# FFN up as seven block products a pair, down summed in PSUM with reloaded features

## What is computed

```python
    h2 = _rmsnorm(x, g_pre_ffn) * (1 + sc2) + sh2
    up = _dwconv_rows(jnp.einsum('bld,df->blf', h2, w_up), conv_w, conv_b, grid)
    ug, uv = jnp.split(up, 2, axis=-1)
    f = jnp.einsum('blf,fd->bld', jax.nn.gelu(ug) * uv, w_down)
    x = x + gt2 * _rmsnorm(f, g_post_ffn)
```

## Time and profile before

| | us |
|---|---|
| three runs, median (lowest to highest) | 1947.3 (1946.1 to 1949.46) |
| the profiled execution | 1945.96 |
| its span, first to last instruction | 1944.2 |
| TensorE busy in it | 1890.8 |
| VectorE, ScalarE, GpSimd busy | 1028.4, 625.3, 86.5 |
| mean granted TensorE clock | 0.994 |

### The profile page before, as it was taken

One profiled execution on the slowest core, in us unless ns is written; L12 is line 12 of the kernel. 1 busy time (PEld: TensorE's weight loads), 2 busy tenths in 40 slices (PEclk: granted clock), 3 DMA queues, 4 the chain that ended last, 5 costly groups with the idle time before them and its releaser, 6 DMA issues.

```text
span 1944.2 us, 25592 instructions
## 1 busy us (share of the span) xinstructions
PE 1890.8 (97%) x10466; PEld 1764.1 (91%) x10466; DVE 1028.4 (53%) x2249; ACT 625.3 (32%) x1125; POOL 86.5 (4%) x125
## 2 busy tenths in 40 slices
PE   7999999999999999999999899999999999999995
PEld 2899999999999999999988899989989989989984
DVE  2662455455555543463545655555555555555557
ACT  3623222323233243451334442322323223223222
POOL 1000000000000100010000100000000000000003
PEclk9999999999999999999999899999999999999998
DMA  9122323223323343383222111111111111111104
GB/s 338 44 83 92 71 78 102 67 91 114 101 73 111 113 105 114 121 281 111 87 98 87 63 46 33 55 34 43 44 44 35 53 44 33 44 35 53 44 33 173
DMA packets 165401, 164.87 MB, mean 85 GB/s; under 512 B 5816, under 2 KB 141524, under 8 KB 165284
## 3 DMA queue, kind: packets, MB, share of 16 engines
q1 hardware_dynamic: 150356, 108.28, 19.0%
q0 software_dynamic: 10432, 37.17, 5.7%
q10 hardware_dynamic: 4496, 17.77, 2.3%
HBM read 131.48 MB, written 31.72 MB: 84 GB/s over the span
## 4 chain that ended last, share of the span: by engine, by line
PE 90%; DVE 6%; ACT 2%; DMA 1%; issue 1%; SPq 0%; ACTq 0%; DVEq 0%
PE ps L707 21%; PE ps L709 21%; PE ps L708 21%; PE ps L962 5%; PE ps L1033 4%; PE ps L1035 4%; PE ps L1034 4%; PE ps L843 2%; PE ps L846 2%; PE ps L845 1%; PE ps L749 1%; DVE H_lo L1468 1%; PE ps L822 1%; DVE acc L1862 1%; PE ps L734 1%; DMA adaw<-in_w_ada_dram 1%
## 5 line engine op out<-in xcount | busy, mean ns | idle before, releaser
L707 PE MATMUL ps<-H_hi,ring_hi 128*128 128x384 f32 x2328 | 797.3, 342 | 6.6 <-DVE H_lo L1468 4.5
L709 PE MATMUL ps<-H_hi,ring_lo 128*128 128x384 f32 x2328 | 779.8, 335 | 0.0
L708 PE MATMUL ps<-H_lo,ring_hi 128*128 128x384 f32 x2328 | 779.7, 335 | 0.0
L707 PEld LDWEIGHTS ps<-H_hi,ring_hi 128*128 128x128 f32 x2328 | 438.3, 188 | 12.0 <-DVE H_lo L1468 6.8
L708 PEld LDWEIGHTS ps<-H_lo,ring_hi 128*128 128x128 f32 x2328 | 438.6, 188 | 1.5
L709 PEld LDWEIGHTS ps<-H_hi,ring_lo 128*128 128x128 f32 x2328 | 438.1, 188 | 0.0
L1840 DVE TENSOR_TENSOR acc<-ps,acc 128x512 f32<-128x512 f32 x198 | 135.1, 689 | 101.5 <-PE ps L1035 101.5
L1468 DVE TENSOR_TENSOR ring_lo<-raw,ring_hi 128x1024 fp32r<-128x1024 f32 (+1 forms) x129 | 152.1, 1188 | 55.9 <-ACT ring_hi L1118 47.3
L1033 PE MATMUL ps<-ring_hi,fT_hi 128*128 128x512 f32 x396 | 156.8, 396 | 10.6 <-DVE acc L1840 8.2
L1034 PE MATMUL ps<-ring_lo,fT_hi 128*128 128x512 f32 x396 | 154.5, 390 | 0.0
L1035 PE MATMUL ps<-ring_hi,fT_lo 128*128 128x512 f32 x396 | 154.5, 390 | 0.0
(11 more groups left out here) (236 smaller groups left out, 1942.4 us busy)
## 6 DMA issues: line engine op xcount, KB each, us to landing
...
```

Of the source, the lines that this page charges most:

```text
L707: pe.matmul(out, whi, xhi, start=first, stop=False)
L708: pe.matmul(out, whi, xlo, start=False, stop=False)
L709: return pe.matmul(out, wlo, xhi, start=False, stop=last)
```

## The change

The weights and activations of one up feature form a product of a 2 x 2 block matrix with a 2 x 2 block matrix: gate and value columns by the two halves of the channels (A11, A12 for gate, A21, A22 for value), and the two halves of the channels by the two halves of the tokens (576 each, `HT`). The last 19 features (`NP`) are made with seven block products in place of eight (Strassen's scheme in Winograd's form). A product has 4 k x 3 matmuls, each over two runs of 288 columns (`SB`) that lie in two neighbouring banks; four such bank pairs are used in turn (`SLOT_BANK`). Features 0 to 2 stay plain products of 384 columns (`PLAIN`).

New work: eight sums of 128x576 for each of four k give the token-side quarters T1 to T4 (`quarter_tiles`, k=3 on VectorE, k=0 to 2 on GpSimd), with hi and lo parts. Four sums of 128x512 a feature give the weight side (`weight_sum`, GpSimd). The seven weights of a pair are split into `up_hi` and `up_lo`, during the pair before. ScalarE copies product 0 out (`hold`), VectorE adds the others to SBUF tiles `held` in seven sums of 576 (`output_sum`). The middle tap (ScalarE, `mid`) and the outer taps (VectorE, two SBUF tiles in) then work on halves of 576 tokens. Gate after gelu and value are stored to DRAM apart (`z_gate`, `z_value`), in four transfers a feature.

Down comes after all of up. For each third of the tokens (r) all 22 features are read back, 384 tokens of gate and of value, and w_down's 128 rows too (so three times in all): VectorE multiplies gate and value and makes the lo parts, ScalarE the hi parts, in rings of four. Three token tiles are summed in three bank pairs over all 22 features without going to SBUF. The last four features of the last third are done tile by tile (`down_end`). The final norm reads PSUM. acc, its memset and the 198 adds are gone. The residual is loaded by GpSimd.

```diff
+PLAIN = 3
+NP = NF - PLAIN
+HT = T // 2
+SB = HT // 2
...
+    SLOT_BANK = (0, 6, 2, 4)
...
+    def product_freed(eng, g):
+
+        s, i = g // 7, g % 7
+        if i == 0:
+            eng.wait_ge(product_held, s + 1)
+        else:
+            eng.wait_ge(output_summed, 7 * s + (i if i < 4 else i + 1))
...
+    def quarter_tiles(eng, done, k, before):
...
+        first, second = slice(0, HT), slice(HT, T)
+        as_f32 = lambda ap: ap.bitcast(F32)
+        x1, x2 = [[as_f32(h[:, k, c]) for h in (H_hi, H_lo)] for c in (first, second)]
+        y1, y2 = [[as_f32(h[:, KD // 2 + k, c]) for h in (H_hi, H_lo)] for c in (first, second)]
+        t1, t2, t3, t4 = [T_full[name][:, k, :] for name in quarters]
+        steps = ((t1, x2[0], x2[1], ALU.add), (t2, y2[0], y2[1], ALU.add), (t3, t2, t1, ALU.subtract),
+                 (t1, t1, x1[0], ALU.subtract), (t1, t1, x1[1], ALU.subtract), (t2, t2, t1, ALU.subtract),
+                 (t4, y1[0], t2, ALU.subtract), (t4, t4, y1[1], ALU.add))
+        for n, (out, a, b, op) in enumerate(steps):
+            if n:
+                eng.wait_ge(done, before + n)
+            eng.tensor_tensor(out, a, b, op).then_inc(done, 1)
...
+            for s in range(NP):
+                if s + 2 < NP:
+                    sp.wait_ge(up_lo_done, 7 * (s + 1))
+                    up_load(s + 2)
+                elif s == NP - 2:
+                    down_load(0)
+                    down_load(1)
+                    f_load(0)
+                else:
+                    down_load(2)
...
-            pool.wait_ge(done2, NT)
-            pool.memset(acc[:, :, :], 0.0).then_inc(acc_zero, 1)
...
+            def weight_sum(s, n):
+
+                a11, a12 = up_raw[s % 2][:, 0, 0:512], up_raw[s % 2][:, 0, 512:1024]
+                a21, a22 = up_raw[s % 2][:, 1, 0:512], up_raw[s % 2][:, 1, 512:1024]
+                if n == 0:
+                    pool.wait_ge(gate_in[s % 2], 16 * (s // 2 + 1))
+                    pool.wait_ge(value_in[s % 2], 16 * (s // 2 + 1))
+                    if s:
+                        pool.wait_ge(up_lo_done, 7 * (s - 1) + 6)
+                    else:
+                        pool.wait_ge(lo_ready, S_FF + 2 * PLAIN)
+                else:
+                    pool.wait_ge(weight_sums, 4 * s + n)
+                if n >= 1:
+                    pool.wait_ge(up_lo_done, 7 * s + ((2, 1, 4) if s else (0, 1, 2))[n - 1])
+                out, a, b, op = ((up_s1[:, :], a21, a22, ALU.add), (a21, a11, a21, ALU.subtract),
+                                 (a11, up_s1[:, :], a11, ALU.subtract), (a12, a12, a11, ALU.subtract))[n]
+                pool.tensor_tensor(out, a, b, op).then_inc(weight_sums, 1)
...
+            pool.wait_ge(h_split_done, 2 * NB * KD)
+            for n, k in enumerate(range(KD // 2 - 1)):
+                quarter_tiles(pool, pool_sums, k, 8 * n)
+                if n == 0:
+                    for j in range(4):
+                        weight_sum(0, j)
+            for s in range(1, NP):
+                for j in range(4):
+                    weight_sum(s, j)
...
+            def product(s, i, xhi, xlo, k0, c0):
...
+                else:
+                    product_freed(pe, g - 4)
+
+                pe.wait_ge(up_lo_done, g + 1)
+                for k in range(KD // 2):
...
+                    for n, (wt, x) in enumerate(((up_hi[i], xhi), (up_hi[i], xlo), (up_lo[i], xhi))):
+                        for sb in range(2):
+                            cols = slice(c0 + sb * SB, c0 + (sb + 1) * SB)
+                            mm = pe.matmul(ps[:, bank + sb, 0:SB], wt[:, w], x[:, k0 + k, cols],
+                                           start=(k == 0 and n == 0), stop=(k == KD // 2 - 1 and n == 2))
+                mm.then_inc(product_done, 1)
+
+            def up_pair(s):
+                product(s, 0, H_hi, H_lo, 0, 0)
+                product(s, 1, H_hi, H_lo, KD // 2, 0)
+                if s == 0:
+                    pe.wait_ge(quarter_lo, KD // 2)
+                product(s, 2, T_hi["T2"], T_lo["T2"], 0, 0)
+                product(s, 3, T_hi["T3"], T_lo["T3"], 0, 0)
+                product(s, 4, T_hi["T1"], T_lo["T1"], 0, 0)
+                product(s, 5, T_hi["T4"], T_lo["T4"], 0, 0)
+                product(s, 6, H_hi, H_lo, KD // 2, HT)
...
+            def down_tile(n, j):
+
+                k, r = down_cell(n)
+                q = TB * r + j
+                bank = SLOT_BANK[(7 * NP + q) % 4]
+                if k == 0:
+                    if q >= 4:
+                        pe.wait_ge(evac2, NT + q - 3)
+                    else:
+                        product_freed(pe, 7 * NP - 4 + q)
+                tok = slice(j * P, (j + 1) * P)
+                for x, w, first, last in ((f_hi, down_hi, True, False), (f_hi, down_lo, False, False), (f_lo, down_hi, False, True)):
...
+                        mm = pe.matmul(ps[:, bank + hb, :], x[n % DR][:, tok], w[n % DR][:, hb * 512:(hb + 1) * 512],
+                                       start=(k == 0 and first), stop=(k == NF - 1 and last))
+                return mm
+
+            def down_feature(n):
+
+                k, r = down_cell(n)
+                pe.wait_ge(down_ready, n + 1)
+                for j in range(TB):
+                    mm = down_tile(n, j)
+                    if k == NF - 1:
                         mm.then_inc(done2, 1)
+                if k < NF - 1:
+                    mm.then_inc(down_used, 1)
+
+            def down_end():
+
+                for j in range(TB):
+                    for n in range(NB * NF - DR, NB * NF):
+                        if j == 0:
+                            pe.wait_ge(down_ready, n + 1)
+                        mm = down_tile(n, j)
+                    mm.then_inc(done2, 1)
 
...
+            for s in range(NP):
+                if s:
+                    second_start(s - 1)
+                up_hi_split(s, 6)
+                next_weights(s, 0)
+                hold(s)
+                if s:
+                    gelu(s - 1, 1)
+                next_weights(s, 1)
+                next_weights(s, 2)
+                act.wait_ge(output_summed, 7 * s + 1)
+                if s:
+                    act.wait_ge(half_stored["g0"], 16 * s)
+                middle_tap(s, "g0", 0)
+                next_weights(s, 3)
+                gelu(s, 0)
+                next_weights(s, 4)
+                act.wait_ge(output_summed, 7 * s + 5)
+                if s:
+                    act.wait_ge(half_stored["v1"], 16 * s)
+                middle_tap(s, "v1", 1)
+                next_weights(s, 5)
...
+                dve.tensor_tensor(split_half(held[out][:, :]), split_half(held[base][:, :]),
+                                  pair_bank(SLOT_BANK[(7 * s + i) % 4]), ALU.add).then_inc(output_summed, 1)
...
+                if n + 1 < NB * NF:
+                    feature_product(n + 1)
+                dve.wait_ge(down_hi_done, n + 1)
+                sub_hi(down_lo[d][:, :], down_raw[d][:, :], down_hi[d][:, :])
+                sub_hi(f_lo[d][:, :], f_raw[d][:, :], f_hi[d][:, :]).then_inc(down_ready, 1)
...
+            plain_up(0, [[2], [3]])
+            quarter_tiles(dve, dve_sums, KD // 2 - 1, 0)
+            plain_up(1, [[4], [5]])
+            for n, k in enumerate((KD // 2 - 1, 0)):
+                quarter_split(k, n)
+            next_weights(-1, 0)
+            next_weights(-1, 1)
+            plain_up(2, [[], []])
+            for i in (2, 3):
+                next_weights(-1, i)
+            for k in range(1, KD // 2 - 1):
+                quarter_split(k, k + 1)
+            for i in (4, 5):
+                next_weights(-1, i)
+            for s in range(NP):
+                if s:
+                    output_sum(s - 1, 5, 5, "v0", "v0")
+                    output_sum(s - 1, 6, 6, "g1", "g1")
+                    outer_taps(s - 1, 3, "v0", 1, 0)
+                up_lo_split(s, 6)
+                if s:
+                    outer_taps(s - 1, 4, "g1", 0, 1)
+                next_weights(s, 0)
+                next_weights(s, 1)
+                output_sum(s, 1, 0, "g0", "g1")
+                output_sum(s, 2, 1, "g1", "g1")
+                next_weights(s, 2)
+                outer_taps(s, 1, "g0", 0, 0)
+                next_weights(s, 3)
+                output_sum(s, 3, 2, "v0", "g1")
+                output_sum(s, 4, 3, "g1", "g1")
+                output_sum(s, 4, 4, "v1", "v0")
+                next_weights(s, 4)
+                outer_taps(s, 2, "v1", 1, 1)
+                next_weights(s, 5)
+            output_sum(NP - 1, 5, 5, "v0", "v0")
+            output_sum(NP - 1, 6, 6, "g1", "g1")
+            outer_taps(NP - 1, 3, "v0", 1, 0)
+            outer_taps(NP - 1, 4, "g1", 0, 1)
 
...
+                dve.scalar_tensor_tensor(out=yo[:, t % 3, :],
+                                         in0=ps[:, bank:bank + 2, :].rearrange("p a b -> p (a b)"), scalar=stat[:, 3, t:t + 1],
```

(1 more changed line is left out.)

577 lines of the change are left out of this document (383 added, 194 removed).

## The result

| | before | after |
|---|---|---|
| median of the runs, us | 1946.8 (4 runs, 1946.1 to 1949.5) | 1883.5 (4 runs, 1881.9 to 1886.7) |
| ratio, 95% interval | | 0.967 [0.966, 0.969] |
| span of the profiled run, us | 1944.2 | 1884.9 |
| TensorE busy, us | 1890.8 | 1839.7 |

The account below looks back on a forecast made before the run. TensorE, busy 97% of the span, was taken as the bound. Start, plain features, quarter wait, half clock, block products, down and tail summed to 1885.7 us of span, giving a 1889 us median; forecast range 1874 to 1902, chance 0.66.

Parts of the forecast that it names:

- The matmuls: Up products on TensorE: 288-column matmuls start every 133.3 ns, so up takes 500.5 us for 549.1, 48.6 saved.
- Both bounds: Limits for one 288-column matmul: 120 ns, columns alone, and 150 ns, from two 128-column matmuls starting 0.15 us apart.
- The memset: Norm before up: without GpSimd's memset of acc, 4.2 us of TensorE wait and 1.8 of clock go, 6.0 in all.
- The road to the third product: Start of up to product 2 of the first pair: TensorE arrives at 1168.2 and waits 13.7 us for the quarters.
- the half clock: After the wait for the quarters, the lowered clock of 0.50 costs TensorE 2.4 us.
- The lower bound: Wait for the quarters before product 2: at least 6 us, ScalarE's and VectorE's own part.
- One pair: Seven products of a feature: TensorE needs 22.4 us, VectorE's loop 21.1, so TensorE sets the pace.
- Rival (a): In the pairs VectorE sets the pace with a loop of 23.6 us: +17, 1906 us; chance 0.14.
- Down: Down stage: 1188 matmuls take 269.3 us, loads charge nothing, two row boundaries cost 1.9 us in both.
- rival (d): SP's loads bound down at 4.5 us a cell: +30 us, 1919 us; chance 0.05.
- The tail: Kernel end behind the last matmul: 11.0 us for 15.5 before, including 6.4 between the last add's end and span's end.
- From span to median: Span of 1885.7 us to median time: 1.8 added for the profiled run over its span, 1.3 for the median above it.

Follow-up runs that it names:

- the last experiment: The changed kernel with the last four down features taken feature by feature over three tiles, not tile by tile: 1890.77 us beside 1883.36 for "after".

## Why the prediction was right, step by step

- **The matmuls.** 133.3 ns by the line was exact: the pair takes 22.40 us, 0.267 us for two matmuls. The saving is 48.7 for the predicted 48.6. Both bounds were off the mark: 120 ignored the 13.3 ns that each width pays, and 150 took two lone matmuls for a floor that lies at 111.6.
- **The memset.** Right in mechanism (the late memset shows it without the rest), 6.9 us for 6.0, and 6.8 alone in the kernel before. I had taken the wait and the clock one by one and assumed that the lower clock behind the norm stays as it was. Whether it does changes from run to run: from 1100 to 1105 us the granted clock is 0.71 in the profiled run of "after" and 1.00 in that of its second measurement.
- **The road to the third product.** From the first block to product 0 it is 63.5 us for 63.6 predicted. TensorE arrives at 1170.8 in its own trace, the wait is 12.1 for 13.7 (the prediction's own 1182.0 - 1168.2 is 13.8), the half clock costs 1.8 for 2.4 (420.97 us from product 2 of the first pair to down, for 3144 x 0.1333 = 419.2). Here the lock is in the trace of "after": four T_lo beside GpSimd's sums took 7.59 us (1168.75), four without took 2.76 (1180.05). The lower bound was the weak point: "ScalarE's and VectorE's own part", 6 us, is 3.2 when the queue is put right, since both work at once.

```profile
1168.75 7.59 DVE L1794 TENSOR_TENSOR T_lo<-T_full,T_hi 128x576 fp32r<-128x576 f32 x4
1180.05 2.76 DVE L1794 TENSOR_TENSOR T_lo<-T_full,T_hi 128x576 fp32r<-128x576 f32 x4 [3.72 <-ACT T_hi L1645]
```

- **One pair.** The loop of 21.1 is 20.7 by the experiment with three extra splits; that with extra sums agrees with this base. VectorE's busy time is 16.25 for the sum's 17.8: I had the single durations right (sum 753 ns for 760, split 687 for 690) and then added time between instructions, where they overlap (1420.40 + 0.69 ends behind 1421.01 above). The waits between dependent steps I had too low by nearly as much (3.3, measured 20.7 - 16.25 = 4.4), so the loop came out right from two errors. Rival (a) stays on the other side by 1.7 us a pair. GpSimd's sums take 1.29 us, not 1.2.
- **Down.** From the first matmul (1603.84) to the end of the last (1875.29) it is 271.45 us for 269.3 + 1.9 = 271.2. The adds went with their waits; TensorE never waited for the loads (242 GB/s at a DMA share of 0.71), so rival (d) has nothing to stand on. Its loads are 524 and 393 KB a cell, 225 GB/s and not 222. The two boundaries show 0.4 us of waits, not 1.9, and the handover from up 0.4 more; 1.35 us of the stretch have no wait in the trace. One reading of before was wrong, though no term hung on it: TensorE did not stand before a down chunk for the feature just made. It stood inside the chunk, ahead of the third half, until VectorE had added the first half to acc and so freed its bank. The trace of before has 4.4 us of this from 1150 to 1850 us, and 3.8 more in the last chunk. Behind the norm it stood for H_lo (1.9), and once for ring_lo (2.5):

```profile
PE ps L1033 <- DVE acc L1840: 4.4, 9, 0.5
```

- **The tail.** 9.6 for 11.0. The row for the stretch behind the last add, 6.4 us in before, is 5.0 here: that term isn't fixed, as the last experiment shows (8.2).
- **From span to median.** I added 1.8 and 1.3 us. The profiled run was itself 3.2 above the median of its four, so this step had the wrong sign here; it can't be told beforehand.

The sum was 1885.7 for a measured span of 1884.9. That closeness is luck: the untouched part ran 3.3 us longer in this run, which covered 0.8 (memset), 1.6 (wait), 0.6 (clock) and 1.4 (tail) of too much cost, less 0.25 in down. Against the median the forecast is 5.5 us high: these 4.2, and the 1.3 that I added for the median.
